# Hybrid encoder block on one core: four column groups of the input projection by Strassen's seven products, in two blocks of 1024 tokens

## What is computed

```python
u = _rmsnorm(h, pre_norm_w[i])                  # 2048 tokens x 1024
proj = u @ w_in[i]                              # 1024 x 4616: nine groups of 512 columns, and 8 gates
sb_q, sb_k, sb_v, sb_z, ml_q, ml_k, ml_v, ml_o, ml_z, ml_i, ml_f = _split_cols(proj)
y_sb = _stick_breaking_attention(...)           # of sb_q, sb_k, sb_v
qk = jax.nn.silu(_causal_conv(jnp.concatenate([ml_q, ml_k], axis=-1), ml_conv_w[i], ml_conv_b[i]))
y_ml = _mlstm_chunkwise(...)                    # of qk, ml_v and the two gates
y = jnp.concatenate([y_sb, y_ml], axis=-1) @ w_out[i]
h = h + _rmsnorm(y, post_norm_w[i])             # then gate * (p[i] @ ple_w_up[i]) is added
```

## Time and profile before

| | us |
|---|---|
| median of 3 runs (1810.32 to 1815.54) | 1813.72 |
| span of the profiled execution, first to last instruction | 1808.6 |
| PE busy | 1761.9 (97%) |
| DVE / ACT / POOL busy | 1119.1 / 991.3 / 680.6 |
| first stage: values' group, 16 token tiles | 0 to 116.6 |
| first stage: groups 0, 1, 4, 5 | 116.6 to 472.3 |
| first stage: gates | 472.3 to 487.3 |

### The profile page before, as it was taken

One profiled execution on the slowest core, in us unless ns is written; L12 is line 12 of the kernel. 1 busy time (PEld: TensorE's weight loads), 2 busy tenths in 40 slices (PEclk: granted clock), 3 DMA queues, 4 the chain that ended last, 5 costly groups with the idle time before them and its releaser, 6 DMA issues. The chain is left out here.

```text
span 1808.6 us, 28177 instructions
## 1 busy us (share of the span) xinstructions
PE 1761.9 (97%) x8972; PEld 1437.3 (79%) x8972; DVE 1119.1 (62%) x1776; ACT 991.3 (55%) x2041; POOL 680.6 (38%) x942
## 2 busy tenths in 40 slices
PE   7999999999899999999999999998999999999998
PEld 6888888878577887888878887886788888788887
DVE  5431214555479898979797979894666666533333
ACT  5431213322277787878787878784677776411111
POOL 1100000000147777777777777772234444200000
PEclk9999999999999999999999999999999999999999
DMA  6677766121394647454656453735555454422220
GB/s 199 163 192 215 232 186 186 52 87 47 126 282 131 172 144 212 135 175 135 174 171 185 135 176 127 249 118 190 169 193 159 162 189 139 162 77 79 81 82 40
DMA packets 193733, 277.05 MB, mean 153 GB/s; under 512 B 66684, under 2 KB 128380, under 8 KB 184408
## 3 DMA queue, kind: packets, MB, share of 16 engines
q1 hardware_dynamic: 190952, 265.19, 47.8%
q0 software_dynamic: 2672, 10.52, 1.7%
HBM read 187.41 MB, written 88.26 MB: 152 GB/s over the span
## 5 line engine op out<-in xcount | busy, mean ns | idle before, releaser
L975 PE MATMUL b_late<-w_split,spare 128*128 128x512 f32 x1416 | 411.4, 415 | 2.5 <-ACT b_p_out L1057 2.3
L756 POOL TENSOR_TENSOR b_a_lo<-b_aT,b_a_hi 128x512 fp32r<-128x512 f32 (+2 forms) x312 | 354.8, 1137 | 25.0
L1138 DVE TENSOR_TENSOR_SCAN b_buf<-b_y,b_buf 128x511 f32<-128x511 f32 (+2 forms) x320 | 357.9, 1118 | 9.1
L529 PE MATMUL a_po<-uT_hi,w_split 128*128 128x512 f32 x1024 | 318.6, 392 | 2.3 <-DVE w_split L397 2.3
L975 PEld LDWEIGHTS b_late<-w_split,spare 128*128 128x128 f32 x1416 | 243.4, 190 | 40.5 <-issue 4.6
L752 POOL CAST b_a_hi<-b_aT 128x512 fp32r<-128x512 f32 (+1 forms) x320 | 182.1, 569 | 179.1 <-PE b_o L949 147.6
L1148 DVE SCALAR_TENSOR_TENSOR b_buf<-b_buf,b_y 128x512 f32<-128x512 f32 (+2 forms) x320 | 187.9, 587 | 70.0 <-PE b_y L935 69.0
L529 PEld LDWEIGHTS a_po<-uT_hi,w_split 128*128 128x128 f32 x1024 | 193.0, 188 | 46.4 <-DVE w_split L397 2.7
L1034 ACT ACTIVATE b_aT<-b_turned 128x512 f32<-128x512 f32 (+1 forms) x320 | 170.3, 532 | 67.6 <-POOL b_a_lo L756 60.1
L529 PE MATMUL a_po<-uT_lo,w_split 128*128 128x512 f32 x512 | 201.6, 394 | 0.0
L1043 ACT ACTIVATE b_buf<-b_y 128x512 f32<-128x512 f32 (+2 forms) x320 | 171.3, 535 | 50.1 <-PE b_y L929 47.7
(11 more groups left out here) (244 smaller groups left out, 3359.6 us busy)
## 6 DMA issues: line engine op xcount, KB each, us to landing
spare<-u_pair SPq DMA_DIRECT2D x62, 1024.0 KB, 5.4
proj_n<-b_p_out SPq DMA_DIRECT2D x59, 256.0 KB, 5.7
c_gates<-proj_n SPq DMA_DIRECT2D x16, 768.0 KB, 4.5
w_raw<-in_w_in POOLq DMA_DIRECT2D x5, 2048.0 KB, 10.1
x_in<-in_x SPq DMA_DIRECT2D x16, 512.0 KB, 3.9
qk_hi<-stage_hi SPq DMA_DIRECT2D x32, 256.0 KB, 2.6
qk_lo<-stage_lo SPq DMA_DIRECT2D x32, 256.0 KB, 2.9
u_pair<-uT_hi SPq DMA_DIRECT2D x16, 512.0 KB, 3.7
```

The costliest lines, as they stand in the source:

```text
L529: mm = pe.matmul(po[t][:], w[:, k, m * P:(m + 1) * P], u[:, k, t * GROUP:(t + 1) * GROUP], start=(k == 0 and n == 0), stop=(k == KT - 1 an ...
L756: nc.gpsimd.tensor_tensor(lo[:, cols], raw, hi[:, cols].bitcast(F32), ALU.subtract).then_inc(lo_done, 1)
L975: mm = pe.matmul(late[:], u_in[f % US][:, u_part, k, :], w[:, k, :], start=(i == 0), stop=(i == PASSES - 1))
L1138: nc.vector.tensor_tensor_scan(down, y[u % YS][:, 1:keys][:, ::-1], down, b[:, keys - 1:keys], ALU.add, ALU.subtract).then_inc(log_done, 1)
```

## The change

Groups 4, 5, 0 and 1 are done in 16 parts (`QUADS`): two blocks of 1024 tokens, and in each block eight pairs of 128-column row tiles. A part is a 2x2 block product, 256 columns by 1024 tokens by a depth of 1024, and Strassen's scheme makes it of seven products (`PRODUCTS`) of half size, each 4 x 3 = 12 matmuls of 128x512, in place of eight. The first four parts of a block go through the convolution, the other four are stored as hi and lo.

The operands on the token side are b11, b12, b21, b22 (quarters of the turned tokens) and t1 to t4, sums of these that DVE and POOL make while the block's second four token tiles are turned (`token_sums`), each split into hi and lo. On the weight side POOL loads 1 MB for each part (`load_pair`), makes s1 to s4 (`weight_sums`) and all seven lo parts (`low`); ACT makes the seven hi parts (`high_op`), slot s for the next part as soon as product s of this one is done. Products add up in three PSUM banks X, Y, Z. X after product 0 is p1 (copied to SBUF by ACT), X after product 2 is the output tile C11; Y after products 1, 3 and 5 is added to p1 by DVE (`u2_done`, `u3_done`, `c21_done`), and Z after products 4 and 6 is added to the sums in place (`c22_done`, `c12_done`).

The values' group and the gates are done within each block, for its eight tiles and its 1024 tokens. The tokens' parts are stored to memory between the products (`store_kept`), and the late group's weights are loaded and split during and behind the last part (`load_late`, `split_late`).

```diff
+        BLOCKS, HALF = 2, 4
+        TILES = 2 * HALF
+        HALO = CONV_K - 1
+        QUADS = [(b, g, h) for b in range(BLOCKS) for g in (4, 5, 0, 1) for h in range(2)]
+        PER = len(QUADS) // BLOCKS
+        SLOTS = len(PRODUCTS)
...
+        def homes(t):
+            j = t % TILES
+            if j < HALF:
+                return u["b11"][:, j], u["b21"][:, j]
+            return b12[:, j - HALF], u["b22"][:, j - HALF]
...
-            for g, columns in enumerate(EARLY[1:] + LATE[:1]):
-                pool.wait_ge(w_lo_done, (g + 1) * KT)
-                pool.dma_start(w_raw[:], w_view[:, :, columns * GROUP:(columns + 1) * GROUP]).then_inc(w_loaded, 16)
...
+            def token_sums(b, i):
+                n = HALF * b + i
+                t2, t3, t4 = (u_plain[k][:, i, 1] for k in ("t2", "t3", "t4"))
+                pool.wait_ge(t2_done, n + 1)
+                pool.wait_ge(u_raw_done, 2 * n + 2)
+                nc.gpsimd.tensor_tensor(t3, t2, u_raw[i][0], ALU.subtract).then_inc(t3_done, 1)
+                nc.gpsimd.tensor_tensor(t4, u_raw[i][1], t2, ALU.subtract).then_inc(t4_done, 1)
...
+            def load_pair(q):
+                b, g, h = QUADS[q]
+                if q % PER == 0:
+                    pool.wait_ge(x_scaled, TILES * (b + 1))
+                    pool.wait_ge(mean_sq_done, TILES * (b + 1))
+                else:
+                    pool.wait_ge(op_lo_done, SLOTS * (q - 1) + 6)
+                first = g * GROUP + h * 2 * P
+                pool.dma_start(raw, w_view[:, :, first:first + 2 * P]).then_inc(w_loaded, 16)
...
+            def weight_sums(q):
+                b = q // PER
+                pool.wait_ge(w_loaded, 16 * (q + 1))
+                if q % PER == 0:
+                    pool.wait_ge(v_stored[0], 16 * HALF * (b + 1))
+                    pool.wait_ge(v_stored[1], 16 * HALF * (b + 1))
+                else:
+                    pool.wait_ge(op_lo_done, SLOTS * q)
+                nc.gpsimd.tensor_tensor(s1, a21, a22, ALU.add).then_inc(w_sum_done, 1)
+                pool.wait_ge(w_sum_done, 4 * q + 1)
+                nc.gpsimd.tensor_tensor(s2, s1, a11, ALU.subtract).then_inc(w_sum_done, 1)
+                nc.gpsimd.tensor_tensor(a21, a11, a21, ALU.subtract).then_inc(w_sum_done, 1)
+                pool.wait_ge(w_sum_done, 4 * q + 2)
+                if q % PER == 0:
+                    pool.wait_ge(v_stored[2], 16 * HALF * (b + 1))
+                    pool.wait_ge(v_lo_done, TILES * (b + 1))
+                nc.gpsimd.tensor_tensor(s4, a12, s2, ALU.subtract).then_inc(w_sum_done, 1)
+            def low(q, s):
+                op = PRODUCTS[s][0]
+                pool.wait_ge(op_hi_done, SLOTS * q + s + 1)
+                nc.gpsimd.tensor_tensor(w_ops[:, s, 1], raw_of[op], w_ops[:, s, 0].bitcast(F32), ALU.subtract)\
+                    .then_inc(op_lo_done, 1)
...
+                for j in range(TILES + 2):
+                    if j + 1 < TILES:
+                        reciprocal_root(TILES * b + j + 1)
+                    if 0 <= j - 5 < HALF:
+                        low_t3(b, j - 5)
+                    if 0 <= j - 4 < HALF:
+                        token_sums(b, j - 4)
+                        low_t2(b, j - 4)
+                q0 = PER * b
+                load_pair(q0)
+                weight_sums(q0)
+                for s in range(SLOTS):
...
+                    act.wait_ge(product_done, SLOTS * (q - 1) + s + 1)
+                act.wait_ge(w_loaded, 16 * (q + 1))
+                if op in ("s1", "s2", "s3", "s4"):
+                    act.wait_ge(w_sum_done, 4 * q + {"s1": 1, "s2": 2, "s3": 3, "s4": 4}[op])
+                nc.scalar.copy(w_ops[:, s, 0], raw_of[op]).then_inc(op_hi_done, 1)
...
+            def copy_c11(q):
+                act.wait_ge(product_done, SLOTS * q + 3)
+                until(act, lo_stored[0], 16 * pairs_before[q])
+                if convs_before[q]:
+                    act.wait_ge(tap_done, 16 * convs_before[q])
+                nc.scalar.copy(c[0][:, HALO:HALO + GROUP], X[:]).then_inc(x_read_act, 1)
...
+                copy_p1(q)
+                silu_before(1)
+                next_op(0)
+                silu_before(2)
+                next_op(1)
+                silu_before(3)
+                if is_conv(q):
+                    copy_c11(q)
+                else:
+                    high_c(q, 0)
+                next_op(2)
+                if q == PER - 1:
+                    square(TILES)
...
+            def convolve(q, n):
+                i, b = CONV_ORDER[n], q // PER
+                m = conv_tile(q, i)
+                before = 4 * convs_before[q] + n
+                source, out = c[i], stage[i][:].bitcast(F32)
+                if i % 2:
+                    nc.vector.tensor_copy(source[:, 0:HALO], c[i - 1][:, GROUP:GROUP + HALO]).then_inc(halo_done, 1)
+                elif b == 0:
+                    nc.vector.memset(source[:, 0:HALO], 0.0).then_inc(halo_done, 1)
+                else:
+                    dve.wait_ge(halo_kept, m + 1)
+                    nc.vector.tensor_copy(source[:, 0:HALO], halo[:, m, :]).then_inc(halo_done, 1)
+                if i % 2 and b == 0:
+                    nc.vector.tensor_copy(halo[:, m, :], source[:, GROUP:GROUP + HALO]).then_inc(halo_kept, 1)
+                dve.wait_ge(halo_done, before + 1)
+                until(dve, hi_stored[i], 16 * q)
+                if i < 2 and q % PER == 0:
+                    dve.wait_ge(gates_stored[i], 16 * (b + 1))
+                nc.vector.tensor_scalar(out, source[:, 0:GROUP], cw[:, m, 0:1], cb[:, m:m + 1], ALU.mult, ALU.add)\
+                    .then_inc(tap_done, 1)
+                for j in range(1, CONV_K):
+                    dve.wait_ge(tap_done, 4 * before + j)
+                    nc.vector.scalar_tensor_tensor(out=out, in0=source[:, j:j + GROUP], scalar=cw[:, m, j:j + 1], in1=out,
+                                                   op0=ALU.mult, op1=ALU.add).then_inc(tap_done, 1)
...
+                conv, last = is_conv(q), q + 1 == len(QUADS)
+                sum_with_p1(q, 1, 1, u2_done)
+                if conv:
+                    dve.wait_ge(x_read_act, convs_before[q] + 1)
+                    convolve(q, 0)
+                else:
+                    low_c(q, 0)
+                if q == PER - 1:
+                    scale(TILES)
+                sum_with_p1(q, 3, 3, u3_done)
...
+            def turn(t):
+                i, b, j = t % 2, t // TILES, t % TILES
+                pe.wait_ge(x_scaled, t + 1)
...
+            def product(q, s):
+                b = q // PER
+                op, home, name, first = PRODUCTS[s]
+                pe.wait_ge(op_lo_done, SLOTS * q + s + 1)
+                if s == 0 and q > 0:
+                    if is_conv(q - 1):
+                        pe.wait_ge(x_read_act, convs_before[q])
+                    else:
+                        pe.wait_ge(c_hi_done, 4 * pairs_before[q - 1] + 1)
+                        pe.wait_ge(c_lo_done, 4 * pairs_before[q - 1] + 1)
+                if s == 1:
+                    until(pe, c21_done, q)
+                if s == 2:
+                    pe.wait_ge(p1_done, q + 1)
+                if s == 3:
+                    pe.wait_ge(u2_done, q + 1)
+                if s == 4:
+                    until(pe, c12_done, q)
+                if s == 5:
+                    pe.wait_ge(u3_done, q + 1)
+                if s == 6:
+                    pe.wait_ge(c22_done, q + 1)
+                if q % PER == 0 and home in ("t1", "t2", "t3", "t4"):
+                    pe.wait_ge({"t1": t1_lo_done, "t2": t2_lo_done, "t3": t3_lo_done, "t4": t4_lo_done}[home], HALF * (b + 1))
+                out = bank[name][:].rearrange("p (s t) -> p s t", s=HALF)
+                for k in range(HALF):
+                    for m, (w_part, u_part) in enumerate(PARTS):
+                        mm = pe.matmul(out, w_ops[:, s, w_part, k, :], u[home][:, :, u_part, k, :],
+                                       start=(first and k == 0 and m == 0), stop=(k == HALF - 1 and m == 2),
+                                       skip_group_check=True)
+                mm.then_inc(product_done, 1)
...
+                for q in range(PER * b, PER * (b + 1)):
+                    for s in range(SLOTS):
+                        if q == PER - 1 and s == SLOTS - 1:
+                            turn(TILES)
...
+PRODUCTS = (("a11", "b11", "x", True), ("s2", "t2", "y", True), ("a12", "b21", "x", False), ("s3", "t3", "y", False),
+            ("s1", "t1", "z", True), ("a22", "t4", "y", False), ("s4", "b22", "z", False))
```

More of the change, by code:

```diff
@@ new lines, in _ @@
+            pe.wait_ge(ident_ready, 1)
+            turn(0)
+            for b in range(BLOCKS):
+                for j in range(1, TILES):
+                    t = TILES * b + j
+                    if t == 1:
+                        values(0, range(HALF))
+                        turn(1)
+                        values(0, range(HALF, KT))
```

(11 more changed lines are left out.)

850 lines of the change are left out of this document (512 added, 338 removed).

## The result

The changed kernel takes 1924.3 us (median of 4 runs, 1923.1 to 1925.3) against 1814.1 for the kernel before (1810.3 to 1815.5): a ratio of 1.062, 95% interval 1.060 to 1.063. It is slower by 110 us where I had forecast 41, and lies outside the range that I gave. The profiled execution took 1925.3 us, with a span of 1923.6.

What follows compares the result with a forecast made beforehand. First stage bound by PE's number of matmuls: -48.2 us saved, +75.6 in two blocks, +8.1 between them, +1 start, +4.9 end gave +41.4 on 1808.6, 1850; as a median 1855, range 1798 to 1880.

Steps and rivals of the forecast that it cites:

- Step (a): Token tiles 4 to 7 of a block: first product's operand late by 10.6 us, 12.7 with the clock.
- the ring: Token tiles 4 to 7: root, scale, low parts and sums tie the engines together, 8.8 us against a tile's 6.49.
- The load D: POOL's load of 1 MB of weights for a part, taken as 6.5 us.
- Step (b): First part of a block: C11's copy behind casts awaiting the load makes product 5 late by 10.1 us, 12.2 with clock.
- Between the blocks: From a block's last product to the next block's tile 8: PE waits 6.0 us uncovered, 8.1 with the clock.
- step (c): Parts 2 to 4: DVE taps colliding with POOL cost PE 3.3 us each, 9.9 a block; part 5 adds 2.
- The clock: PE runs at half rate (1.2 GHz level) after a stall of some us, charged 2.1 us beyond the stall.
- The chain's own length: DVE's work from the end of product 5 to the sum for the next product 3: about 10.8 us against 11.0.
- The end: PE's idleness before the attention's first score: 12.5 us against 7.6, so 4.9 more.
- rival B: No change: no collisions, but D of 7.0 and more; 37 us for two blocks, +2.4, 1816; chance 0.11.
- A: Rival, faster: no collisions, taps run while POOL waits for its load, D is 5.5; -11.4, 1802; chance 0.28.
- C: Rival, much slower: each POOL operation delays a tap, 9.8 us a part in place of 3.3; 1894; chance 0.07.

Runs made afterwards that it cites:

- experiment three: Changed kernel, but in each block's first part ACT copies C11 ahead of the casts of the next part: 1909.6 us.
- experiment two: Changed kernel, but the convolution's taps add up in four idle PSUM banks, where SiLU reads them, in place of SBUF: 1855.8 us, ratio 1.024 to before.
- Experiment one: Changed kernel, but POOL's seven low parts of the weights become memsets that read nothing: 1888.3 us.
- experiment nine: Changed kernel with taps in PSUM, product 3's sum and a block's first weight load earlier, C11 copied earlier in first two parts, its tap wait relaxed: 1827.6 us.

## Why the prediction was wrong

**What held.** The counts and the pace: 192 matmuls fewer, and undisturbed parts of 19.0 us. Step (a): 1.25 and 3.55 us before tiles 6 and 7 are turned and 5.74 before product 0 make 10.5, predicted 10.6 (10.1 in block 1), and the product behind takes 5.04 in place of 2.88 us. From the end of tile 4's turning POOL issues the load at 36.8 us, predicted 35.6, so the ring was right and not only its sum. The load D is 6.1, taken as 6.5. Step (b): 7.6 and 9.4 us before product 5, predicted 10.1, by the mechanism named (experiment three). Between the blocks: 5.54, predicted 6.0. PE's timeline and the DMA's issues (KB each, us to landing):

```profile
58.66 1.81 PE L790 MATMUL a_pt<-a_ident,w_ops_plain 128*128 128x128 f32 x8 [3.55 <-DVE u_t_plain L621]
...
85.47 5.04 PE L863 MATMUL a_x<-u_b,w_ops 128*128 128x512 f32 x12 [5.74 <-POOL w_ops L272]
...
301.38 1.94 PE L790 MATMUL a_pt<-a_ident,w_ops_plain 128*128 128x128 f32 x8 [5.54 <-DVE u_b L609]
```

```profile
w_raw<-in_w_in POOLq DMA_DIRECT2D x17, 1024.0 KB, 6.1
```

**What failed is step (c), the price of a convolution part: 3.3 us, measured 9.7 to 11.7.** The four parts behind a convolution part in block 0 start at 116.80 and end at 234.70: 117.9 us for 4 x 19.04, 41.7 too much; those of block 1 (406.17 to 527.85) are 45.5 too much. Both together are 87 us, where step (c) with its part 5 had 3 x 3.3 + 2 in a block, 23.8. That is 63 of the 74 us by which the sum was short (a span of 1923.6 against 1850). Of the 87 us 65.9 are the eight waits before product 3, and 19 more are the products behind them, which take 4.4 to 5.5 us each in place of 2.88. Step (c) had the right place and the right cause, and two of its terms were wrong:

- The collisions on the chain. By rows 7 a tap lost 0.21 us, and 3.3 us was to be the price of the whole part. Measured, a tap loses 0.50 on average (1.248 against 0.752), a first tap 0.38, and the one or two three-column copies of a chain that meet a POOL operation 1.1 each; first taps and copies I had put at nothing. And I let the 23.3 us of both engines spread over a part of 19.2, though POOL's operations lie in one row just where DVE's chain is. In the changed kernel the chain takes 18.6 us in block 0 and 18.9 to 19.3 in block 1; free of collisions it would take an estimated 11.4 (the 12.2 of experiment two, less 0.8 for its first taps). So they stretch it by 7.2 to 7.9 us, and experiment two takes 5.3 to 6.5 of these away.
- The clock. I charged 2.1 us only for the stalls of (a), (b) and the change of blocks, and none in (c); only the range had up to 15 us for the clock after small stalls. There it was lost behind each of the eight waits of 7.9 to 8.7 us.

The chain's own length was nearly right: 10.8 us of work for 11.0, estimated above at 11.4 for 10.9. The text names four convolved tiles in it, but 10.8 is the sum of three tiles, three sums and 0.3 for the rest, and three tiles stand there.

The Trainium skill (SBUF — State Buffer, section Who interferes with whom) states, beside the rule on two SBUF inputs that the prediction used, that copies and `tensor_scalar` can enter a mode that takes both port pairs, and then exclude GpSimd too. The trace agrees: 0.55 to 1.45 us for the first tap and 0.17 to 1.24 for the copy beside POOL, and 0.81 for the first tap, beside POOL or not, with its output in PSUM. I had read the one rule and passed over the other. It also says that a GpSimd instruction that only writes leaves a VectorE instruction with two SBUF inputs alone. Experiment one agrees: 0.752 us for the 22 taps beside memsets alone. The exclusion for a whole instruction, which the prediction took from there, does not add up to the time measured: by it a tap and a POOL operation in turn would take 0.75 + 1.27, some 2.0 us, and in the row of three taps from 127.13 a turn comes every 1.67.

**The end** was the other miss: 17.8 us of idle time, forecast 12.5.

```profile
592.51 1.27 SPq L354 DMA_DIRECT2D qk_lo<-a_c  x1
602.07 0.45 SPq L1041 DMA_DIRECT2D qst_hi<-qk_hi  x1
...
608.13 0.45 PE L1273 MATMUL b_y<-spare,qst_lo 128*128 128x128 f32 x1 [17.83 <-DMA qst_lo<-qk_lo]
```

I had counted DVE's work and the queries' load, not the landing of the last low store between them: issued at 592.51, it lets SP go on at 602.07 only (SP waits 7.2 us for it by the profile). The gates' stores had that place before. This is 5 us more than forecast, and parts 6 to 8 are another 6: they cost 3.0 and 5.3 us beyond their matmuls in the two blocks, where I had 1 in each.

**Two slips in the sums.** The 5.1 us between the profiled span and the median, which I carried over from the kernel before, are 0.7 here. And rival B's terms add up to +2.8, not +2.4.

**The rivals.** A and B needed taps without collisions, and fell with L701's 1.248 us. C, which I gave 7 in 100, had the right order: 9.8 us a part against 9.7 to 11.7, and 1894 against 1924. That the price of a part came out so near is in part luck, since 2 to 3 us of the measured one are the clock, which C does not have, and since not every tap is delayed. What I held against it, that POOL is idle for five of 19 us, was right as a count: 26 of 96 taps meet no POOL operation. But each of the other 70 loses 0.68 us, not the 0.21 of rows 7.

## What to carry to other kernels

Where a chain on one engine has to fit between two matmul groups, list it operation by operation, and price each with the time that it takes beside what the other engine does at that very moment; a comparison of busy times over the whole stretch says nothing about it. An accumulation on VectorE beside a busy GpSimd is worth trying in PSUM if banks are free: in this kernel this alone gave back 68 of 110 us, though each first tap got 0.27 us longer. And a wait that was removed by a new order comes back at the next consumer as long as the queue is as long as before (7.95 us before product 3, 7.82 before product 5), so shorten the queue first and then order it.

## What the runs showed that I had not expected

A DVE copy of three columns takes 1.24 us beside a POOL sum and 0.17 without, and 0.44 beside a memset. A memset leaves the taps with two SBUF inputs at 0.752 us, while one first tap (one SBUF input, SBUF output) that met a sum and four memsets in a row took 3.27 in place of 0.55. And a long wait of PE costs more than itself: behind the waits of 7.6 to 9.4 us the next product took 4.4 to 5.5 us in place of 2.88, behind those of up to 1.5 us 3.0; behind waits of 1.8 to 2.8 us it was 3.0 or 4.2 to 4.6 (1.98 and 2.69 us with 3.0 in the changed kernel, 1.81 and 2.65 with 4.58 in experiment nine).
